# Two-scalar scaling on GpSimd for the softmax weights of three mixers, with a new table of step places for all five

## What is computed

```python
# mixer D (differential attention), 4 heads of two maps, every query sees all 512 keys
p = jax.nn.softmax(sc, axis=-1)
w = (p[:, :, 0] - lam * p[:, :, 1]).astype(v.dtype)
return jnp.einsum('bhqs,bshe->bqhe', w, v)
# mixers L (MLA, 8 heads) and G (GQA, 4 x 2 jobs)
s = jnp.einsum('bqhgd,bshd->bhgqs', qb, k).astype(jnp.float32) * scale
p = jax.nn.softmax(s, axis=-1).astype(v.dtype)
return jnp.einsum('bhgqs,bshe->bqhge', p, v)
```

## Time and profile before

| | us |
|---|---|
| median of 3 runs (lowest, highest) | 3045.55 (3044.97, 3048.2) |
| the profiled execution: its own time | 3042.94 |
| its span in the trace | 3041.1 |
| TensorE, VectorE, ScalarE, GpSimd busy | 2862.1, 1663.6, 1142.6, 184.9 |

### The profile page before, as it was taken

One profiled execution on the slowest core, in us unless ns is written; L12 is line 12 of the kernel. 1 busy time (PEld: TensorE's weight loads), 2 busy tenths in 40 slices (PEclk: granted clock), 3 DMA queues, 4 the chain that ended last, 5 costly groups with the idle time before them and its releaser, 6 DMA issues.

```text
span 3041.1 us, 33674 instructions
## 1 busy us (share of the span) xinstructions
PE 2862.1 (94%) x13182; PEld 2348.3 (77%) x13182; DVE 1663.6 (55%) x2508; ACT 1142.6 (38%) x1766; POOL 184.9 (6%) x178
## 2 busy tenths in 40 slices
PE   6987889999999999999789999999999887799999
PEld 5766778888887888887678888888887665688887
DVE  6586644564555444446954444543444987644443
ACT  4455543332224222243643232432223776432322
POOL 1012310000000000001200000000000321000000
PEclk9888899999999999999899999999999999999999
DMA  3111013333323333232013333233322010123232
GB/s 127 63 43 43 11 52 97 111 97 97 98 90 96 99 95 100 85 103 70 14 56 97 97 97 94 91 100 97 97 89 63 30 42 21 35 90 104 91 97 84
DMA packets 70542, 240.50 MB, mean 79 GB/s; under 512 B 7888, under 2 KB 9808, under 8 KB 70128
## 3 DMA queue, kind: packets, MB, share of 16 engines
q1 hardware_dynamic: 68112, 230.85, 24.4%
q0 software_dynamic: 1120, 5.39, 0.5%
q10 hardware_dynamic: 1152, 2.10, 0.2%
HBM read 236.21 MB, written 2.10 MB: 78 GB/s over the span
## 4 chain that ended last, share of the span: by engine, by line
PE 84%; DVE 10%; ACT 3%; issue 3%; POOL 0%; DMA 0%; DVEq 0%; ACTq 0%; POOLq 0%
PE ps L284 83%; DVE SC L307 2%; DVE SM L313 2%; PE ps L287 1%; DVE PTL L295 1%; DVE SC L295 1%; ACT SC L292 1%; DVE SC L301 1%; DVE WL L295 1%; DVE SC L310 0%; DVE SM L321 0%; DMA PR<-par 0%; POOL SC L302 0%; DVE EQ L295 0%; DVE SC L302 0%
## 5 line engine op out<-in xcount | busy, mean ns | idle before, releaser
L284 PE MATMUL ps<-HH,WH 128*128 128x512 f32 (+1 forms) x2192 | 860.0, 392 | 14.6 <-DVE HL L307 14.2
L284 PE MATMUL ps<-HH,WL 128*128 128x512 f32 (+1 forms) x2192 | 856.7, 391 | 0.0
L284 PE MATMUL ps<-HL,WH 128*128 128x512 f32 (+1 forms) x2192 | 856.4, 391 | 0.0
L295 DVE TENSOR_TENSOR WL<-WF,WH 128x1024 fp32r<-128x1024 f32 (+2 forms) x473 | 545.5, 1158 | 417.0 <-ACT WH L292 416.3
L292 ACT ACTIVATE WH<-WF 128x1024 fp32r<-128x1024 f32 (+2 forms) x473 | 467.5, 994 | 702.3 <-PE ps L284 702.2
L284 PEld LDWEIGHTS ps<-HH,WH 128*128 128x128 f32 (+1 forms) x2192 | 413.5, 189 | 103.7 <-issue 14.6
L284 PEld LDWEIGHTS ps<-HH,WL 128*128 128x128 f32 (+1 forms) x2192 | 412.9, 188 | 87.3
L284 PEld LDWEIGHTS ps<-HL,WH 128*128 128x128 f32 (+1 forms) x2192 | 413.2, 189 | 86.2
L284 PE MATMUL ps<-AH,WH 128*128 128x512 f32 x880 | 342.7, 389 | 3.9 <-DVE AL L295 3.9
L284 PE MATMUL ps<-AL,WH 128*128 128x512 f32 x880 | 342.4, 389 | 0.0
L284 PE MATMUL ps<-AH,WL 128*128 128x512 f32 x880 | 342.3, 389 | 0.0
(11 more groups left out here) (282 smaller groups left out, 3148.3 us busy)
## 6 DMA issues: line engine op xcount, KB each, us to landing
WF<-wall SPq DMA_DIRECT2D x397, 512.0 KB, 3.5
WF<-wall SPq DMA_DIRECT2D x40, 384.0 KB, 3.0
WF<-wall SPq DMA_DIRECT2D x17, 256.0 KB, 2.7
X<-xT ACTq DMA_DIRECT2D x8, 256.0 KB, 12.2
outT<-X POOLq DMA_DIRECT2D x8, 256.0 KB, 2.3
WF<-wall SPq DMA_DIRECT2D x4, 288.0 KB, 3.0
LT<-late POOLq DMA_DIRECT2D x1, 1152.0 KB, 5.6
LP<-latep POOLq DMA_DIRECT2D x1, 1024.0 KB, 7.3
```

Source lines behind the costliest of these rows:

```text
L284: return self.real.matmul(o, l, r, start=start, stop=stop, skip_group_check=True)
L295: return self.real.tensor_tensor(o, a, b, op) if self.real is not None else Uncounted()
```

## The change

Two edits. First, the scaling of *normed* moves in D, L and G from VectorE to GpSimd, in the form with two scalars: in L and G the second scalar is a column of ones, in D it is lambda, so that the product of the reciprocal with lambda falls away. VectorE keeps the reciprocals, in D also the joining, which becomes a stage of its own (*joined*). N and M keep their engines.

Second, `in_turn` reads its tables in another way: the first number is a lag in fractions of an item, the second a slope by which the four blocks T of a job are set apart; and all six tables have new numbers. `BLOCKWISE` is set twice in the file; when the lists are made the second one holds, so *joined* has no slope.

```diff
@@ -201,46 +201,56 @@
...
 G_PLACE = {
-    "made": (0, 10), "largest": (1, 0), "raised": (1, 3), "normed": (2, 2), "turned": (2, 19), "high": (3, 7),
...
+    "made": (0.323, -0.202), "largest": (1.689, -0.051), "raised": (2.374, 0.255), "normed": (3.929, -0.199),
...
+BLOCKWISE = ("decays", "m_made", "made", "largest", "raised", "normed", "joined", "turned", "high", "low")
+
+
 def in_turn(place, *items):
 
-    due = sorted(((i + place[name][0] + delay, place[name][1], i, n, key) for i, item in enumerate(items)
-                  for n, (name, delay, key) in enumerate(item)), key=lambda d: d[:4])
-    names = [[name for name, _, _ in item] for item in items]
-    return [(names[i][n], key) for _, _, i, n, key in due]
+
+
+
+    due = []
+    for i, item in enumerate(items):
+        for n, (name, delay, key) in enumerate(item):
+            lag, slope = place[name]
+            block = key[1] if name in BLOCKWISE else 0
+            due.append((round(i + lag + delay + slope * block, 4), i, n, name, key))
+    return [(name, key) for *_, name, key in sorted(due, key=lambda d: d[:3])]
+
+
+BLOCKWISE = ("decays", "m_made", "made", "largest", "raised", "normed", "turned", "high", "low")
...
-def attend(job, T, end=()):
-    core = ("made", "largest", "raised", "normed", "turned", "high", "low")
+def attend(job, T, end=(), core=("made", "largest", "raised", "normed", "turned", "high", "low")):
     return [(s, 0, (job, T)) for s in core] + ([(s, 0, job) for s in end] if T == 3 else [])
...
-        items += [attend(h, T, NORMED) for T in range(4)]
+        items += [attend(h, T, NORMED, ("made", "largest", "raised", "normed", "joined", "turned", "high", "low"))
+                  for T in range(4)]
     return in_turn(D_PLACE, *items)
...
 def sc_drops(ph, stage, key):
-    if ph == "D" and stage in ("normed", "turned"):
-        return [(ph, "P1" if stage == "normed" else "P0", key)]
+    if ph == "D" and stage in ("joined", "turned"):
+        return [(ph, "P1" if stage == "joined" else "P0", key)]
...
 def sm_drops(ph, stage, key):
     if ph == "D" and stage == "normed":
+        return []
+    if ph == "D" and stage == "joined":
         return [(ph, "m1", key), (ph, "m0", key)]
...
-            "P": (turned, "turned"), "P0": (turned, "turned"), "P1": (normed, "normed"), "y": (pooled, "added"),
+            "P": (turned, "turned"), "P0": (turned, "turned"), "P1": (normed, "joined"), "y": (pooled, "added"),
...
-            "m": (normed, "normed"), "m0": (normed, "normed"), "m1": (stepped, "second"), "r": (widened, "widen"),
+            "m": (normed, "normed"), "m0": (normed, "joined"), "m1": (pooled, "normed"), "r": (widened, "widen"),
...
-            if ph == "N" and kind == "m":
+            if ph in "NLG" and kind == "m":
                 return [pooled[ph, "normed", key]]
...
-                    e.wait_ge(*(pooled if ph == "N" else normed)[ph, "normed", key])
+                    e.wait_ge(*(normed[ph, "joined" if ph == "D" else "normed", key] if ph in "MD" else pooled[ph, "normed", key]))
...
             for stage, key in order["D"]:
-                rope_stage("D", stage, key)
+                if stage == "normed":
+                    P, sm = tile("D", "P1", key), small("D", "m1", key)
+                    e.wait_ge(*stepped["D", "inverse1", key])
+                    e.wait_ge(*stepped["E", "lam"])
+                    e.wait_ge(*pooled.so_far())
+                    e.tensor_scalar(P, P, sm[:, 2:3], LM[:, 5:6], ALU.mult, ALU.mult).then_inc(*pooled("D", "normed", key))
+                else:
+                    rope_stage("D", stage, key)
             e.wait_ge(*projected[piece["fd"][fpieces[5][1] + 23]])
             e.dma_start(LT[:, :], late).then_inc(s_late, 16)
-            for stage, key in order["L"]:
-                rope_stage("L", stage, key)
-            for stage, key in order["G"]:
-                rope_stage("G", stage, key)
+            for ph in "LG":
+                for stage, key in order[ph]:
+                    if stage == "normed":
+                        P, sm = tile(ph, "P", key), small(ph, "m", key)
+                        e.wait_ge(*stepped[ph, "normed", key])
+                        e.wait_ge(*pooled.so_far())
+                        e.tensor_scalar(P, P, sm[:, 2:3], cc("ones")[:, 0:1], ALU.mult, ALU.mult)\
+                         .then_inc(*pooled(ph, "normed", key))
+                    else:
+                        rope_stage(ph, stage, key)
...
                 elif stage == "normed":
-                    sm, P = small(ph, "m", key), tile(ph, "P", key)
+                    sm = small(ph, "m", key)
                     e.wait_ge(*raised[ph, "raised", key])
                     e.reciprocal(sm[:, 2:3], sm[:, 1:2]).then_inc(*stepped(ph, "normed", key))
-                    if ph != "N":
-                        e.wait_ge(*stepped[ph, "normed", key])
-                        e.tensor_scalar(P, P, sm[:, 2:3], None, ALU.mult).then_inc(*normed(ph, "normed", key))
...
                 elif stage == "normed":
                     sm0, sm1 = small("D", "m0", key), small("D", "m1", key)
-                    P0, P1 = tile("D", "P0", key), tile("D", "P1", key)
                     e.wait_ge(*raised["D", "raised1", key])
                     e.reciprocal(sm1[:, 2:3], sm1[:, 1:2]).then_inc(*stepped("D", "inverse1", key))
-                    e.wait_ge(*stepped["D", "inverse1", key])
-                    e.wait_ge(*stepped["E", "lam"])
-                    e.tensor_tensor(sm1[:, 3:4], sm1[:, 2:3], LM[:, 5:6], ALU.mult).then_inc(*stepped("D", "lam", key))
-                    e.wait_ge(*stepped["D", "lam", key])
-                    e.tensor_scalar(P1, P1, sm1[:, 3:4], None, ALU.mult).then_inc(*stepped("D", "second", key))
                     e.reciprocal(sm0[:, 2:3], sm0[:, 1:2]).then_inc(*stepped("D", "inverse", key))
+                elif stage == "joined":
+                    P0 = tile("D", "P0", key)
                     e.wait_ge(*stepped["D", "inverse", key])
-                    e.scalar_tensor_tensor(P0, P0, sm0[:, 2:3], P1, ALU.mult, ALU.subtract).then_inc(*normed("D", "normed", key))
+                    e.wait_ge(*pooled["D", "normed", key])
+                    e.scalar_tensor_tensor(P0, P0, small("D", "m0", key)[:, 2:3], tile("D", "P1", key), ALU.mult, ALU.subtract)\
+                     .then_inc(*normed("D", "joined", key))
```

More of the change, by code:

```diff
@@ L203 @@
 Q_PLACE = {
[L204 removed]
+    "q_source": (0.2, 0), "q_take": (2.0, 0), "q_conv": (2.03, 0), "q_bent": (3.02, 0), "q_parts": (4.01, 0),
 }
 M_PLACE = {
[L207 to L209 removed]
@@ L214 @@
+    "x_made": (1.311, -0.066), "x_first": (2.052, 0.171), "x_bent": (2.486, -0.052), "x_turned": (3.733, 0.155),
+    "x_kept": (3.791, -0.094), "x_second": (4.343, -0.12), "x_ended": (6.105, 0.085),
 }
 N_PLACE = {
-    "made": (0, 18), "largest": (1, 0), "raised": (1, 9), "normed": (2, 1), "turned": (2, 22), "high": (4, 5),
-    "low": (4, 11), "product": (5, 19), "source": (0, 20), "take": (1, 2), "rot": (2, 25), "squares": (2, 6),
-    "roped": (3, 8), "added": (3, 10), "sums": (2, 27), "root": (3, 15), "widen": (4, 4), "spread": (4, 21),
@@ L219 @@
-    "scaled": (5, 3), "done": (6, 24), "half1": (6, 7), "half2": (7, 13), "parts": (8, 14), "c_made": (0, 16),
-    "c_largest": (0, 17), "c_raised": (2, 12), "c_normed": (3, 17), "c_turned": (3, 26), "c_kept": (4, 23),
+    "made": (2.137, -0.007), "largest": (4.332, 0.027), "raised": (4.696, 0), "normed": (5.693, -0.014),
+    "turned": (5.792, 0.306), "high": (7.61, -0.028), "low": (7.716, 0.012), "product": (8.785, 0.047),
+    "source": (1.409, 0.014), "take": (2.878, -0.158), "rot": (6.22, -0.146), "squares": (5.151, -0.051),
@@ new lines @@
+    "joined": (2.426, 0.087), "turned": (2.82, 0), "high": (3.633, -0.036), "low": (3.872, -0.062),
+    "product": (4.747, 0.346), "source": (0.406, 0.269), "take": (1.118, 0.035), "rot": (2.431, -0.463),
+    "squares": (1.945, -0.094), "roped": (3.112, 0.037), "added": (4.749, -0.154), "sums": (2.893, 0.112),
+    "root": (4.305, 0.006), "widen": (4.659, 0.059), "spread": (5.782, 0.187), "scaled": (6.315, 0.132),
+    "done": (7.039, -0.052), "h_squares": (5.494, -0.013), "h_take": (7.376, -0.299), "h_sums": (6.285, -0.049),
@@ L229 @@
+    "h_root": (7.461, 0.422), "h_widen": (7.928, -0.106), "h_spread": (8.747, -0.34), "h_scaled": (9.856, -0.207),
+    "s_product": (0, -0.18), "s_gated": (1.206, -0.016), "s_parts": (4.847, -0.309),
 }
 L_PLACE = {
-    "made": (0, 18), "largest": (1, 2), "raised": (1, 4), "normed": (2, 3), "turned": (2, 20), "high": (4, 0),
-    "low": (4, 9), "product": (5, 19), "source": (0, 12), "take": (1, 17), "rot": (2, 23), "squares": (2, 10),
-    "roped": (3, 8), "added": (4, 13), "sums": (2, 24), "root": (3, 6), "widen": (4, 7), "spread": (5, 21),
@@ L234 @@
-    "scaled": (6, 5), "done": (8, 16), "half1": (6, 1), "half2": (6, 11), "parts": (9, 14), "v_turned": (2, 22),
-    "v_parts": (4, 15),
```

(15 more changed lines are left out.)

29 lines of the change are left out of this document (15 added, 14 removed).

## The result

The changed kernel took **3015.3 us** (median of 4, 3014.2 to 3022.4) beside 3045.3 us for the kernel before on the same chip: a ratio of 0.9905 (95% interval 0.9888 to 0.9923), 30 us less. The forecast was 3001.5 in a range of 2962 to 3036: the sign and the range held, the gain was two thirds of the 44 us. One execution of e11 (3274 us, clock 0.83) and one of the kernel before beside e9 to e11 (5759 us) were slow and enter no number here.

The account below looks back on a forecast made before the run. TensorE bounds the kernel, but in the mixers it waits for scalings, and VectorE sets the pace in D and L. M 0, N -12, D -7, L -9, G -16 sum to -44 us: forecast 3001.5, range 2962 to 3036.

Parts of the forecast that it names:

- M, forecast 0: Mixer M: fewer scores ahead, but TensorE full in a piece and the tail's chain kept; 0 us, bounds -6 to +6.
- a window over 133 us: Mixer M: sign of a wrong forecast, meaning that its shorter distance costs something after all.
- the distance: TensorE: scores of later blocks between a block's scores and its transpose; M 1.4 to 0.75, D unchanged at 1.4.
- -20 at the transposes: Mixer N: one more block ahead covers 20 of the 27.3 us that transposes wait for GpSimd's scaling.
- +8: Mixer N: cover shrinks by two steps, so 16 products may each lose 0.5 us, 8 us in all.
- The round trip through GpSimd: Mixer D: the scaling now goes through GpSimd and back, on the path of the transposes; D -7, bounds -13.5 and +4.
- relief and order: Mixer L: net VectorE relief 13.4 us; TensorE becomes the next bound, product loses a step (+3); -9 in all.
- The term for the transposes: Mixer G: -10 of the 12.1 us that the transposes wait for VectorE's scaling.
- The stretch: VectorE slowed 0.31 us per us of new GpSimd work: 7.6 us in L and in G, 3.8 in D.
- the slower rival: Each of 80 scalings holds VectorE for its whole 0.772 us, order gives nothing: +8.4, 3054 us; chance 0.09.
- All waits go: Rival: all waits on the scaling go in N, G, L and D, plus some clock: -90, 2955 us; chance 0.10.
- no change: Rival: freed time returns as equal waits at the GpSimd queue, within 0.2% of 3045.5 us; chance 0.06.

Follow-up runs that it names:

- e11: M's x steps alone in their new order, the rest of M old, against e8; 3007.3 us, M 128.7 us.
- e9: M's attention steps with product and head norms in their new order, ropes and x steps old, against e8; 3013.5 us, M 136.9 us.
- e6: Changed kernel with M's transpose of a block's weights 0.47 of a place later; 3024.1 us, M 147.8 us.
- e12: Against e8, only M's block steps in their new order, and N's last rope step at 9.40; 3006.4 us, M 124.2 us.
- e1: Changed kernel with mixer M in its old order; 3008.3 us, ratio 0.9884, M 125.8 us.
- e2: Kernel before with only mixer M in its new order; 3061.0 us, ratio 1.0059, M 140.7 us.
- e5: Changed kernel run again, unedited; 3020.5 us beside 3042.0 for the kernel before, ratio 0.9919, M 137.7 us.
- e3: Changed kernel with the scalings of D, L and G back on VectorE and M in its old order; 3031.4 us, ratio 0.9957.
- e4: Kernel before with the scalings of D, L and G on GpSimd, every mixer in its old order; 3049.6 us, ratio 1.0026.
- e8: e1 with VectorE's reciprocal in G placed earlier, at 3.35 for every block; 3003.9 us, ratio 0.9872, G 100.9 us.

## Why the prediction was right, and where it was wrong

**M, forecast 0, came out at +14.4 and +10.2**, past its bounds of 6, and the sign named for it, a window over 133 us, came. The step that failed was "fewer scores ahead, but TensorE is 10.00 of 10 us busy in a piece of its first part, and the tail's chain stays". The tail did stay. But TensorE without idle time was not TensorE safe from the order: new places opened short stops, and the clock, which the sum held at nothing, took more than they did. Of the 14.4 us 10.2 are the same matmuls at a lower clock and 4.2 idle time; in front of product 4 the clock's share follows stops, in front of products 2 and 3 it came without any. My own first explanation, the distance, did not stand either: e6 restored it without gain, e12 shortened it without loss. What is shown: M's order costs 10 to 16 us of the M window (e1, e2, e5), most of it ahead of products 3 and 4, as stops of 1 to 2 us and more time at the lower clock, and no one of the groups tried carries all of it. Which pair of steps makes the stops, and what lowers the clock where there are none, stays open.

**N, -12 against -8.7 and -13.6.** -20 at the transposes was -22. +8 was set aside for the products, whose cover shrinks by two steps; they lost nothing (2.0 and 1.9 us). In its place came 11.3 us for copies, 8.9 of them for that of yk, a wait that I did not look for, though the rope's last step had also been moved later. The two terms were wrong by about as much in opposite ways, so it is luck that the sum of N came near.

**D, -7 against -10.7.** VectorE's busy time between the stage's marks fell from 91.07 to 78.44 us, 12.6, all of the 12.3 us of work removed (13.5 with its gaps): no stretch is seen here, where 3.8 had been charged. The transposes' wait for the combination fell from 19.4 to 8.2 us, and one of 4.2 us stands at a matmul. The round trip through GpSimd cost nothing that can be seen. The prediction says that the order on TensorE is the same in D. That is wrong: scores, transposes and products keep their order, and so the distance of 1.4 is right, but the steps of the ropes and norms between them moved, and VectorE's order changed too. The order alone gave 3.6 us (e3).

**L, -9 against -7.4.** VectorE 141.9 to 127.2 us is 14.7 less, 13.4 were forecast. But the sum treated relief and order as two terms that add, and e3 and e4 show each alone as a loss. So it is luck that L's number came near.

**G, -16 against -8.3 and -5.8.** VectorE fell by 11.2 us (11.3 forecast), and the low parts' wait by more than forecast (15.9 to 2.4 between the marks, -6 forecast). The term for the transposes failed: forecast -10, came out +8 (10.3 to 18.6). 3.1 scores of later blocks ahead of a transpose do not help while the reciprocal that releases GpSimd stands late on VectorE (e8).

**The stretch.** GpSimd's scaling took 768 ns in D as forecast, but 882 in L and 851 in G. VectorE's groups in L of the changed kernel, against the earlier trace rows:

```profile
L317 DVE SCALAR_TENSOR_TENSOR SC<-SC,PR,LT 96x512 f32<-96x512 f32 x16 | 19.9, 1241 | 0.0
L320 DVE COPY SC<-SM 128x384 f32<-128x384 f32 x16 | 13.0, 811 | 0.5
```

The stretch went to the rope product (891 to 1241 ns, 16 times, 5.6 us), not to the copy, which I had named. In all, L's VectorE was relieved of 20.9 us of scalings and fell by 14.7: 6.2 us of stretch for 32 scalings, 0.19 us each, where 0.24 was forecast and the slower rival needed 0.67. In G it was 5.6 us, and 4.6 of it in six low parts of Q, before and after:

```profile
L295 DVE TENSOR_TENSOR GQ<-SC,GQ 64x512 fp32r<-64x512 f32 x6 | 5.3, 880 | 2.4 <-ACT GQ L292 2.4
```

```profile
L305 DVE TENSOR_TENSOR GQ<-SC,GQ 64x512 fp32r<-64x512 f32 x6 | 9.9, 1643 | 0.2
```

The size was near, but the term, so much stretch for each us of GpSimd's work, is not what the runs show. With the same scalings on GpSimd in the old order (e4) these two instructions take 868 and 879 ns, and with the new order and no scalings there (e3) 869 and 696 ns. The rope product of L in e4:

```profile
L306 DVE SCALAR_TENSOR_TENSOR SC<-SC,PR,LT 96x512 f32<-96x512 f32 x16 | 13.9, 868 | 0.0
```

VectorE fell there by 19.4 us in L for the 20.9 removed. So the stretch comes with the move and the new places together, and not with the move as such. That the places do it by what they put beside a scaling is argued, not shown.

The slower rival is out by its mechanism. The Trainium skill (SBUF — State Buffer, Who interferes with whom) says that the port pair which VectorE and GpSimd share is an exclusive lock, and that a VectorE instruction with two inputs from SBUF contends with a GpSimd instruction that reads SBUF. The two stretched instructions, both with two inputs from SBUF, agree with it in kind; on average over the scalings in L they lose a fifth of one (0.19 of 0.88 us). A kernel slower than before did appear, e4, by another mechanism, the hop without the distance, which the prediction priced nowhere. *All waits go* and *no change* did not come. The range was said to leave out some 0.1 above; by the chances given it left out 0.15, the 0.09 of the slower rival and the 0.06 of no change.

## What to carry to other kernels

Moving a step to an idle engine and giving it room in the order are one change: here the first alone cost 6 us, the second alone gave 12, both gave 35. When an order is made anew for all stages, time each stage apart, and keep the old order where the new one loses. A stage in which the first engine shows no idle time is not safe from a new order: here M lost 4 us to new idle time and 10 to the clock. Give the granted clock a term of its own in the sum, and read it in the rows of more than one execution.
